# Decode and prefill layer on one core: x and parameters issued by SP, masks between the page fetches, the memory projections' banks, and cache pages in 8 KB pieces

## What is computed

```python
p = x @ w_in                     # (264, 1024) @ (1024, 6912): q, k, v, q_mem, p_rw, three gates
# stick-breaking attention; a sample token looks at 2048 cached positions in 16 pages of 128
z = (q . k_cache[page_table]) * 0.125 + bias          # 8 heads of 64
log_keep = log_sigmoid(-z)
w = exp(log_sigmoid(z) + sum of log_keep over all LATER positions)
o_sb = w @ v_cache[page_table]
# attention to 256 memory tokens: softmax; prompt keys and values are mem_prompt @ w_mem_kv,
# those of the sample requests are cached
# RWKV-7 recurrence on p_rw; sigmoid gates; output projections; layer norm
# mixture of 32 experts, top 4 (w_gate_up 1024x2048, w_down 1024x1024 each); layer norm
```

## Time and profile before

| | |
|---|---|
| median of three runs | 1644.68 us (1643.41 to 1649.91) |
| the profiled execution's own time | 1647.71 us, its span 1646.0 us |
| TensorE busy | 1508.7 us (92%) |
| VectorE, ACT, GpSimd busy | 590.6, 271.1, 149.6 us |
| DMA | 534.10 MB, 324 GB/s on the mean |
| mean granted TensorE clock | 0.961 |

### The profile page before, as it was taken

The page is one execution under the profiler, slowest core; times in us unless marked ns, Lnnn a source line. Parts: engine busy times, 40 slices in busy tenths (PEclk is TensorE's granted clock), DMA queues, the critical chain, the costliest instruction groups (busy, mean ns, idle before and its releaser), DMA issues.

```text
span 1646.0 us, 21021 instructions
## 1 busy us (share of the span) xinstructions
PE 1508.7 (92%) x7762; PEld 797.0 (48%) x7762; DVE 590.6 (36%) x961; ACT 271.1 (16%) x535; POOL 149.6 (9%) x271
## 2 busy tenths in 40 slices
PE   6995897879899979799999999999999999999993
PEld 5884553448788864543443344343333334334331
DVE  1799853457455544221211212121221211212124
ACT  1101141132221211211110111111011111111102
POOL 5522132211120010000000000000000000000000
PEclk9998899979899979799999999999999999999997
DMA  8898789892310115499999999999999999999991
GB/s 303 285 347 311 249 314 330 318 321 103 78 46 7 52 62 228 168 420 427 429 428 429 429 428 428 429 428 428 428 429 428 428 428 430 428 428 428 430 428 42
DMA packets 83913, 534.10 MB, mean 324 GB/s; under 512 B 8639, under 2 KB 9722, under 8 KB 59282
## 3 DMA queue, kind: packets, MB, share of 16 engines
q1 hardware_dynamic: 59314, 467.69, 69.0%
q0 software_dynamic: 14144, 45.79, 8.4%
q10 hardware_dynamic: 10400, 19.92, 3.4%
HBM read 528.91 MB, written 4.46 MB: 324 GB/s over the span
## 4 chain that ended last, share of the span: by engine, by line
PE 54%; DMA 30%; DVE 7%; issue 5%; POOL 1%; SPq 1%; ACT 1%; POOLq 0%; ACTq 0%; DVEq 0%
PE bank L747 52%; DMA projT<-in_w_gate_up 26%; DVE ring L1850 4%; PE bank L748 2%; DMA ring<-in_cache_sb_v 2%; DMA ring<-in_cache_mem_k 1%; DMA ring<-in_cache_mem_v 1%; DVE sample_logits L1856 1%; DMA arena<-in_x_sample 1%; DVE arena L2160 0%; DVE arena L2252 0%; POOL arena L627 0%; DMA ring<-in_cache_sb_k 0%; DVE arena L2103 0%; DVE arena L2405 0%
## 5 line engine op out<-in xcount | busy, mean ns | idle before, releaser
L747 PE MATMUL bank<-arena 128*128 128x128 f32 (+9 forms) x2172 | 335.0, 357 | 15.4 <-DVE arena L2286 4.5
L747 PEld LDWEIGHTS bank<-arena 128*128 128x128 f32 (+4 forms) x2172 | 229.3, 182 | 130.3 <-issue 116.6
L747 PE MATMUL bank<-ring,memT 128*64 128x512 f32 (+2 forms) x1152 | 282.8, 599 | 8.7 <-ACT memT L1790 7.6
L747 PE MATMUL bank<-projT,ring 128*128 128x264 f32 x1056 | 256.5, 398 | 4.1 <-DVE projT L2169 2.7
L2344 DVE TENSOR_SCALAR arena<-bank 128x256 f32<-128x256 f32 x64 | 26.9, 420 | 636.9 <-PE bank L747 636.9
L747 PE MATMUL bank<-projT 128*64 128x512 f32 (+1 forms) x1056 | 232.8, 586 | 9.3 <-DMA projT<-in_w_gate_up 9.2
L747 PE MATMUL bank<-ring,projT 128*64 128x512 f32 x1024 | 230.3, 597 | 0.0
L747 PEld LDWEIGHTS bank<-projT,ring 128*128 128x128 f32 x1056 | 202.5, 196 | 42.7 <-issue 4.0
L747 PEld LDWEIGHTS bank<-ring,memT 128*64 128x64 f32 (+2 forms) x1152 | 85.2, 139 | 156.6 <-issue 138.5
L747 PEld LDWEIGHTS bank<-projT 128*64 128x64 f32 (+1 forms) x1056 | 75.5, 138 | 161.3 <-issue 133.8
L747 PEld LDWEIGHTS bank<-ring,projT 128*64 128x64 f32 x1024 | 69.3, 137 | 147.4 <-issue 147.4
(11 more groups left out here) (272 smaller groups left out, 912.8 us busy)
## 6 DMA issues: line engine op xcount, KB each, us to landing
ring<-in_w_gate_up SPq DMA_DIRECT2D x64, 2048.0 KB, 22.1
projT<-in_w_gate_up SPq DMA_DIRECT2D x64, 2048.0 KB, 24.5
ring<-in_w_down SPq DMA_DIRECT2D x64, 2048.0 KB, 20.4
ring<-in_cache_sb_k SPq DMA_DIRECT2D x64, 256.0 KB, 5.3
ring<-in_cache_sb_k POOLq DMA_DIRECT2D x64, 256.0 KB, 5.3
ring<-in_cache_sb_v SPq DMA_DIRECT2D x64, 256.0 KB, 5.2
ring<-in_cache_sb_v POOLq DMA_DIRECT2D x64, 256.0 KB, 5.5
ring<-in_w_in ACTq DMA_DIRECT2D x7, 2048.0 KB, 13.9
```

Source lines behind the costliest of these rows:

```text
L747: mm = lambda out, l, r, first, last, **k: pe.matmul(out, l, r, start=first, stop=last, **k)
```

## The change

1. **SP issues x and all parameters.** x_prompt and x_sample come first on SP's queue, before the page table and w_in block 0; mem_prompt and the 13 small DMAs stand behind w_in block 0. GpSimd issues none of them.
2. **GpSimd's masks.** Pages of units 0 to 3 come right behind `ident`; the small masks follow; then units 4 to 9, `m_page`, units 10 to 15, `m_mem[0]`, units 16 to 21, `m_mem[1]`, units 22 to 31.
3. **Banks and order.** The first selection product takes bank 5, `mv` banks 4 and 0, and `q_broadcast(("qb", 7))` stands behind `mv`.
4. **Pages in 8 KB pieces.** Page j of a unit goes to the partitions j, j+4, j+8, ... (32 of them), four consecutive positions (8 KB) on each. The q and t axes of a unit now mean "position 4a+t of page j on partition 4a+j".
5. **The sum over later positions** follows that layout: three linked adds within a partition's four positions (`own`), three over the four units of a request (`spx` is a quarter as large), a product of 128 columns with a matrix `later`, another of 128 with `ones`, and one more add of 384 numbers for the own later positions. `later` is made once: GpSimd builds `in_order` and `turned_ge` (a memset and two selects), TensorE multiplies them in front of chunk 2, ACT moves the result.

```diff
@@ psum_plan
+            add("later", 2)
-    add(("cs_s", 0), 0)
-    add(("qb", 7), 7)
+    add(("cs_s", 0), 5)
     for h in range(MH):
         add(("mk", h), h)
     for tt in range(2):
-        add(("mv", tt), 4 + tt)
+        add(("mv", tt), (4, 0)[tt])
+    add(("qb", 7), 7)
@@ build
-        spx = ar(1024, 4, PAGES, SBH)
+        spx = ar(1024, 4, PAGES // 4, SBH)
+        in_order, turned_ge, later = ar(5200, P), ar(5400, P), ar(12880, P)
@@ fetch_pages
-                eng.dma_start(unit(name)[:, j, :], src[bass.ds(page, 1), :, :].rearrange("g p n -> p (g n)")).then_inc(
+                at_, c0 = page_place(name), 2048 * (page_place(name) % 2)
+                eng.dma_start(ring[j:P:4, 2 + at_ // 2, c0:c0 + 2048], src[bass.ds(page, 1), :, :].rearrange("g (p t) n -> p (g t n)", t=4)).then_inc(
                     sem(landed_sem), 16)
@@ sync: first of all
+            sp.dma_start(xr[:, 0:2, :], xs).then_inc(sem("x_in"), 16)
+            sp.dma_start(xr[0:NB, 2, :], A["x_sample"].rearrange("b s d -> (b s) d")).then_inc(sem("x_in"), 16)
             sp.dma_start(pages[:], A["page_table"].rearrange("b n -> (b n)").unsqueeze(0)).then_inc(sem("pages_in"), 16)
@@ sync: mem_prompt, prow, shrow, sb_bias, w_lora, w_gate2 moved here from gpsimd
             load_columns(sp, ("win", 0))
+            sp.dma_start(memr[:, :, :], A["mem_prompt"][0].rearrange("(t p) d -> p t d", p=P)).then_inc(sem("mem_in"), 16)
...
             sp.wait_ge(sem("pages_in"), 16)
@@ gpsimd
+            paged = lambda m: m.rearrange("p (a q) -> p q a", q=4)
+            link(g.memset(in_order, 0.0))
+            link(g.affine_select(out=paged(in_order), in_=paged(in_order), compare_op=ALU.not_equal, fill=1.0, base=0,
+                                 pattern=[[-32, 4], [-1, 32]], channel_multiplier=1))
+            sel(paged(turned_ge), paged(ones[:]), ALU.is_ge, 0, [[-32, 4], [-1, 32]], 1)
             g.sem_inc(sem("tri_ready"), 1)
...
-            for u in range(4, 8):
-                second_half(("K", u))
...
+            for u in range(4, 10):
+                second_half(("K", u))
+            own_rows(m_page[:], 40, 0, SBH)
+            for u in range(10, 16):
+                second_half(("K", u))
+            own_rows(m_mem[0], 36, 0, MH)
+            for u in range(16, 22):
+                second_half(("K", u))
+            own_rows(m_mem[1], 36, 16, MH)
             g.sem_inc(sem("masks"), 1)
-            for u in range(8, 32):
+            for u in range(22, 32):
                 second_half(("K", u))
@@ tensor, in front of chunk 2
+                    pe.wait_ge(sem("tri_ready"), 1)
+                    b = start("later")
+                    done("later", mm(b[:, 0:P], in_order, turned_ge, True, True))
@@ selection_sums
-                mm(b[:, :], tri_ge[:], sb_, True, False)
-                done(("cs_s", i), mm(b[:, :], ones[:], spx.rearrange("p b n h -> p (b n h)"), False, True))
+                mm(b[:, 0:P], later, sb_.rearrange("p (a t h) -> p a t h", t=4, h=SBH)[:, :, 3, :], True, False)
+                done(("cs_s", i), mm(b[:, 0:P], ones[:], spx.rearrange("p b n h -> p (b n h)"), False, True))
@@ page_softplus
-                spv = sb_.rearrange("p (b n h) -> p b n h", b=4, n=PAGES)
-                for n in range(PAGES - 2, -1, -1):
-                    ins = tt_(spx[:, :, n, :], spx[:, :, n + 1, :], spv[:, :, n + 1, :], ALU.add)
+                own = sb_.rearrange("p (a t h) -> p a t h", t=4, h=SBH)
+                for t in range(1, 4):
+                    link(tt_(own[:, :, t, :], own[:, :, t, :], own[:, :, t - 1, :], ALU.add))
+                sums = sb_.rearrange("p (b n t h) -> p b n t h", b=4, n=4, t=4)[:, :, :, 3, :]
+                for n in range(2, -1, -1):
+                    ins = tt_(spx[:, :, n, :], spx[:, :, n + 1, :], sums[:, :, n + 1, :], ALU.add)
...
+                z4 = half_of(i).rearrange("p (a t h) -> p a t h", t=4, h=SBH)
+                link(tt_(z4[:, :, 1:4, :], z4[:, :, 1:4, :], own[:, :, 0:3, :], ALU.add))
```

More of the change, by code:

```diff
@@ L469, in _ @@
         def _(sp):
+            xs = A["x_prompt"][0].rearrange("(t p) d -> p t d", p=P)
+            sp.dma_start(xr[:, 0:2, :], xs).then_inc(sem("x_in"), 16)
+            sp.dma_start(xr[0:NB, 2, :], A["x_sample"].rearrange("b s d -> (b s) d")).then_inc(sem("x_in"), 16)
             sp.dma_start(pages[:], A["page_table"].rearrange("b n -> (b n)").unsqueeze(0)).then_inc(sem("pages_in"), 16)
@@ L493, in _ @@
             load_columns(sp, ("win", 0))
+            sp.dma_start(memr[:, :, :], A["mem_prompt"][0].rearrange("(t p) d -> p t d", p=P)).then_inc(sem("mem_in"), 16)
+            vec = lambda n, k: A[n].rearrange("l (t p) -> (l t) p", p=P)
+            r0 = 0
+            for n, k in (("mu_rw", 14), ("w_decay0", 4), ("w_aaa0", 4), ("rw_k_k", 4), ("rw_k_a", 4)):
+                sp.dma_start(prow[r0:r0 + k, :], vec(n, k)).then_inc(sem("param_in"), 16)
+                r0 += k
+            sp.dma_start(prow[r0:r0 + 4, :], A["rw_r_k"].rearrange("l (t a) d -> (l t) (a d)", a=2)).then_inc(sem("param_in"), 16)
+            r0 += 4
+            for n in ("rw_gn_g", "rw_gn_b"):
+                sp.dma_start(prow[r0:r0 + 4, :], vec(n, 4)).then_inc(sem("param_in"), 16)
+                r0 += 4
+            sp.dma_start(shrow[0:NB, :], A["state_rw_shift"][0]).then_inc(sem("param_in"), 16)
+            sp.dma_start(sb_bias[:], A["sb_bias"][0].partition_broadcast(P)).then_inc(sem("bias_in"), 16)
+            sp.dma_start(w_lora[0:64, :], A["w_decay2"][0]).then_inc(sem("lora_in"), 16)
+            sp.dma_start(w_lora[64:128, :], A["w_aaa2"][0]).then_inc(sem("lora_in"), 16)
+            sp.dma_start(w_gate2[:], A["w_gate2"][0]).then_inc(sem("lora_in"), 16)
             sp.wait_ge(sem("pages_in"), 16)
@@ L563, in _ @@
             g.sem_inc(sem("ident_ready"), 1)
[L564 to L576, removed]
-            g.dma_start(w_lora[0:64, :], A["w_decay2"][0]).then_inc(sem("lora_in"), 16)
-            g.dma_start(w_lora[64:128, :], A["w_aaa2"][0]).then_inc(sem("lora_in"), 16)
-            g.dma_start(w_gate2[:], A["w_gate2"][0]).then_inc(sem("lora_in"), 16)
             def second_half(name):
@@ L622, in _, with own_rows @@
             sel(pick4[:], pick4[:], ALU.is_ge, 31 - 128, [[32, 12]], -1)
-            for m, step, offs, n in [(m_page[:], 40, 0, SBH), (m_mem[0], 36, 0, MH), (m_mem[1], 36, 16, MH)]:
+            def own_rows(m, step, offs, n):
                 link(g.memset(m, 0.0))
@@ L709, in _ @@
             g.dma_start(brt, A["b_router"][0].partition_broadcast(P)).then_inc(sem("ln_in"), 16)
-            g.dma_start(xres[:, 0:2, :], xs).then_inc(sem("ln_in"), 16)
+            g.dma_start(xres[:, 0:2, :], A["x_prompt"][0].rearrange("(t p) d -> p t d", p=P)).then_inc(sem("ln_in"), 16)
             g.dma_start(xres[0:NB, 2, :], A["x_sample"].rearrange("b s d -> (b s) d")).then_inc(sem("ln_in"), 16)
@@ L823, in _ @@
                 done(("mv", tt), last)
+            q_broadcast(("qb", 7), Q0, NP_TOK + 7)
             for ft in range(K0, K0 + 8):
@@ L1555, in _ @@
                     move("shift_in", shT[:].rearrange("p t b -> p (t b)"), lambda b: b[:, 0:RWT * NB])
+                    move("later", later, lambda b: b[:, 0:P])
                 move(("p", ft), pT[:, ft, :], lambda b: b[:, 0:T])
```

12 lines of the change are left out of this document (6 added, 6 removed).

## The result

The changed kernel takes 1638.41 us in the median of six runs (1630.63 to 1644.88), the kernel before beside it 1647.3 us (six runs, 1643.11 to 1651.15): a ratio of 0.9937, interval 0.9912 to 0.9961. It is faster by 8.9 us where 19 was forecast, and its runs lie 14 us apart. The profiled execution is its slowest, 1644.88 us with a span of 1643.2; a second profile of the same kernel comes further down.

What follows compares the result with a forecast made beforehand. Bound: a TensorE and VectorE chain up to the merged tokens, then expert loads at full DMA. 15.9 us before unit 28 plus 3 behind make 19 off 1647.7: 1628.7; less 3.0 to the median, 1625.7, said as 1625 (1609 to 1640).

Steps and rivals of the forecast that it cites:

- The start: First transposes and w_in products on TensorE: x issued first brings the first products to 14.2 us, a gain of 4.6 us.
- Hidden, by some 2 us: w_in block 1 lands about 30 us, before TensorE wants it at 32.6, so it costs no wait.
- The masks and the sums: On VectorE: all 8.56 us of idle before unit 8 go; sums fall from 3.35 to 2.1 us, gaining 1.2 twice.
- The banks: Ahead of unit 28: TensorE's 22.6 us bank wait goes; unit 28 starts at 172.1, still waiting 5.8, 15.9 us earlier.
- at 14 it is there at 141.6: Block 0 of w_mem_kv, issued at 127.6, lands in 14 us, some 5 us after TensorE's last work.
- The V units: TensorE's dense stretch behind unit 31: 1.6 + 4 - 2.5 = 3 us gained (-1 to 15).
- The term of 4 us for cheaper pages: V stretch: 8 KB pieces cost less engine time, so 4 (0 to 12) of 12.3 us of TensorE's DMA-related waits go.
- the 2.5 against them: V stretch: 2.5 us charged for slower matmuls after TensorE stands idle some 14 us before it.
- Weights starve: Rival, 13%: larger page pieces take more turns, blocks land in 17 us, 13 of the 19 us go: 1639.
- A page on 32 partitions is slower: Rival, 12%: pages written to 32 partitions move at 249 GB/s, K and V units lengthen: 1679, or 1662 in between.
- The V stretch's waits go too: Rival, 16%: behind unit 31, 12 us of waits and some 3 of slow clock go, not 4: 1614.
- The form does nothing, only the order gains: Rival inside the forecast, no chance of its own: the pages' 8 KB form gains nothing, 15.9 + 1.6 - 2.5, so 1629.7.

Runs made afterwards that it cites:

- e10: Changed kernel with request 7's broadcast directly behind the first selection product, and mem_prompt and 13 small DMAs behind w_in block 1: 1628.5 us, ratio 0.9874.
- e2: Kernel before with only the 8 KB page layout and its sums: 1646.3 us, ratio 0.9997.
- e7: Kernel before with only the bank plan and the broadcast for request 7 behind the memory values: 1639.4 us, ratio 0.9954.
- e8: Changed kernel with GpSimd fetching one of its two pages for K units 4 to 27, a quarter of their cached keys left out: 1625.7 us, ratio 0.9873.
- e3: Changed kernel with the broadcast for request 7 back between memory keys and memory values: 1628.6 us, ratio 0.9903.
- e9: Changed kernel with the broadcast for request 7 directly behind the first selection product, ahead of the memory keys: 1629.7 us, ratio 0.9890.
- e1: Changed kernel with the old page layout (2 KB pieces on 128 partitions) and the old sums: 1633.6 us, ratio 0.9901.
- e5: Changed kernel with 2 KB pages, the old sums, and the broadcast for request 7 between memory keys and values: 1632.5 us, ratio 0.9922.
- e11: e10 with pages in 2 KB pieces and the old sums: 1627.9 us, ratio 0.9876.
- e4: Changed kernel with all four pages of a unit issued by SP, none by GpSimd: 1680.8 us, ratio 1.0207.

## Why the forecast was right in direction and wrong in size

The forecast was 15.9 us up to the copy, 3 behind it, and 3.0 off the sum because the profiled execution before lay so far over the median. Measured were 2.3 and 15.0 us up to the copy in two profiles, +0.5 and -0.8 behind it, and 8.9 in the median. The 3.0 stood on three runs; the median of six is 1647.3, so that step alone puts 2.6 us into the distance between 1625 and 1638.4.

**The start: 4.6 us forecast, 4.6 measured at 14.2 us, and 1.5 to 3.2 of it left at unit 4** (57.18 before, 53.99 and 55.72 in the two profiles). "Hidden, by some 2 us" was wrong: block 1 was to land at 30 us and landed at 34.0 in both profiles. The sum had counted 5.8 MB on SP's queue alone; between 11 and 34 us GpSimd's queue moved 2.10 MB more on the same engines, which were full there (363 GB/s at a share of 1.01). At 365 GB/s that is 5.8 us, enough for the 4 us that were missing. Moving 1 MB behind block 1 (e10) starts unit 4 1.1 to 3.3 us sooner than in the kernels with the old place.

**The masks and the sums: right.** No idle stretch ahead of unit 8, and 2.2 us for the sums.

**The banks: right in kind, and here stands the step that failed:** "at 14 it is there at 141.6", and for the w_in blocks no wait at all. Of this the first profile shows the cost. Block 0 of w_mem_kv was issued at 137.4 and not at 127.6, and landed 17.3 us later: 154.7. Of those 9.8 us, 7.0 are waits for w_in blocks and 2.3 the slower chunk behind the longest of them; the landing adds 3.3. The forecast took the landings from a trace in which VectorE stood still for 8.56 us, and from a stretch whose engines were at 1.00. The same edit that removes the pause makes the pages be fetched without one. Then the stage wants 1.05 MB in 4.52 us of pages and 2.1 MB in 15.1 us of weights, 232 + 139 = 371 GB/s, and between 72 and 116 us the rows of the nine profiles without the pause and with pages on two queues show 352 to 390 at shares of 0.95 to 1.05: next to nothing to spare.

How much the pause was worth is less sure than this sounds, since VectorE runs without one from 84 us on in the kernel before as well. The two w_in blocks issued between 80 and 103 us landed after 16.6 us on the mean in those nine profiles (12.0 to 22.1), after 14.5 in the three that keep the pause (before, e2, e7: 11.5 to 18.0), and after 12.4 in e8. The direction is that of the explanation, the ranges overlap, and what makes one landing of the same kernel 12 us and the next 17 or 22 stays open. With less demand (e8) the blocks land in 9.9 to 13.8 us and the median is 1625.7, where 1625 was forecast, though by another way: the copy is at 185.6 and not at 190.

**The order made it dear.** With the broadcast behind the memory values, a late w_mem_kv goes to VectorE: it waits 18.06 us in one profile, 3.62 in the other. e3 and e9 remove that wait and gain 17.4 and 17.2 us over the kernel before, where the changed kernel gains 8.9; part of this is the 5.8 us of wait that the forecast itself had in its chain. e8 keeps the order, has the loads in time, and gains 21.2, some 2 of them behind the copy. So the chain from late loads through TensorE to unit 28 is what was missing; the forecast had seen the chain but taken its loads as sure. How the 8.9 us of the median divide between the start, the w_in blocks and w_mem_kv isn't measured, as only two executions have a profile. Why each kernel scatters as it does isn't settled: e8, where the engines have room, stays within 2.9 us, but so do e7 and e9, and e10 does not.

**The V units: +3 forecast, 0 measured.** TensorE's waits there, 186 to 352 us:

```profile
PE bank L765 <- DMA ring<-in_cache_sb_v: 7.8, 3, 6.3
PE bank L765 <- DVE ring L1982: 4.0, 1, 4.0
```

7.8 and 4.0 us against 8.7 and 3.6 in the earlier trace rows. From the copy to the end of the span it takes 1439.9 us before, 1439.4 and 1440.7 after, 1440.1 in e2, 1442.6 in e1. The term of 4 us for cheaper pages fails by its own reason: nearly all of the wait for V pages stayed. The 1.6 us of the smaller selection product and the 2.5 against them can't be seen singly. The whole gain is made ahead of the copy.

**The rivals.** *Weights starve* gave 1639, and the time is 1638.4, but that nearness is partly luck. Its effect came: in the first profile blocks land after 17 to 22 us and TensorE waits 15.1 us for them where it said 13; in the second it waits 4.9. Its cause, the longer pieces, isn't shown and isn't refuted: with 2 KB pieces (e1, e5, e11) TensorE waits for weights as well. The block issued at 81 and 82 us took 17.4 us with 2 KB pages (e11) and 16.0 with 8 KB (e10); but the one behind it took 13.7 to 16.7 in the six profiles with 2 KB pages on two queues and 15.5 to 22.1 in the six with 8 KB ones and the full demand. In time there is no difference (e10, e11). The Trainium skill (DMA: Bandwidth & Descriptors, "Queues, rings and completion order") has each engine go round the queues and change only after a whole packet; no run here shows that, and none separates the queues' turns from the plain lack of rate, and e4, meant for that, met SP's issue limit first. *A page on 32 partitions is slower* fell: the engine time per MB went down, from 3.02 to 2.82 us, by this row of GpSimd's queue in the changed kernel.

```profile
q0 software_dynamic: 8976, 43.05, 7.4%
```

The Trainium skill's formula for the ports (SBUF — State Buffer, "Door 1: The DMA port swizzle") gives a step of four partitions all 16 of them; the trace agrees so far as these 2.82 us show no slowing, the ports themselves aren't in it. *The V stretch's waits go too* fell with the waits for V pages above, 7.8 us for 8.7. *The form does nothing, only the order gains* is what e2 and e11 say of the time, and its 1629.7 is within 1.2 us of e3's and e10's, whose order isn't the one it priced.

## What to carry to other kernels

Before a load is called hidden, add up the bytes of every queue that moves in that stretch, not only of its own. Before a stall is booked as a gain, ask what was not being fetched while the engine stood; if the DMA engines are at 1.00 beside it, add up the stretch's bytes per period anew, and take a landing time of the old trace as one value of a wide range. In a full stretch, place work that only waits for on-chip data ahead of work that waits for a load, above all on the engine whose order others hang on. And where landings decide, one profile of a kernel is one draw: two of the same kernel here differ by 11.4 us, and the rows trace that to a few landings.

## What the runs showed of the hardware

- Three queues, two with pages in 2 KB or 8 KB pieces and one with weight blocks, moved 352 to 390 GB/s between 72 and 116 us at shares of 0.95 to 1.05 (nine profiles); the 2 MB loads of the expert stage 428. A 2 MB block issued behind 45 us landed after 9.9 to 13.8 us where 313 GB/s were asked for (e8), and after 11.4 to 22.1 us where it was 371 (the changed kernel, two profiles).
- Pages of 32 pieces of 8 KB on every fourth partition cost 2.80 to 2.82 us of the 16 engines per MB, 128 pieces of 2 KB 3.00 to 3.02.
- SP issues one 256 KB page, its address read from a register, every 1.26 us (0.47 us of it in the DMA instruction), which caps a stream of such pages from this queue alone at about 208 GB/s (e4).
- How long TensorE stood doesn't by itself tell how slow the next 64 matmuls are. After 4.40 us they took 16.77 us at a granted clock of 0.86 (changed), but these two rows, of e2 and then of e3, have the slow chunk behind the shorter wait; the granted clock is 0.89 in the first and 1.00 in the second.

```profile
120.07 16.17 PE L755 MATMUL bank<-projT,ring 128*128 128x264 f32 x64 [1.22 <-DMA ring<-in_w_in]
```

```profile
117.03 14.51 PE L765 MATMUL bank<-projT,ring 128*128 128x264 f32 x64 [2.71 <-DMA ring<-in_w_in]
```
